# Even layer of a diffusion backbone: two modulation vectors summed over row chunks on VectorE, first attention scores inside the last value block

## Chip, cores and metric

One core of a Trainium2 chip runs the whole kernel in one launch. The metric is the device time of that launch in microseconds (us), median of the runs. The engines are TensorE (PE in the profile), VectorE (DVE), ScalarE (ACT), GpSimd (POOL) and SyncE (SP), which here only issues transfers.

## The reference

Two trunk layers over 256 latent and 256 context tokens of width 1024, all in float32. Each layer is a mixer and then a hierarchical mixture of 32 experts (top 2). Both take their input normalised, scaled and shifted by modulation vectors, and their output is multiplied by a gate vector. There are six vectors a layer, for each of the two streams:

```python
mx = jnp.split((silu_c @ w_mod[l] + b_mod[l])[:, None, :], N_MOD, axis=-1)   # latent stream, c
mc = jnp.split(silu_cc @ w_mod[l] + b_mod[l], N_MOD, axis=-1)                # context stream, c_ctx
hx = rmsnorm(x, norm_mix[l]) * (1.0 + mx[1]) + mx[0]
y_x, y_c = even_mixer(hx, hc, ...)
x = x + mx[2] * y_x
hx = rmsnorm(x, norm_ffn[l]) * (1.0 + mx[4]) + mx[3]
```

`w_mod[l]` is 1024 x 6144, so one vector is a product of two rows (silu of c and of c_ctx) with a 1024 x 1024 matrix of 4 MiB. The even mixer (layer 0) projects `hx` into queries, keys, values and the two halves `u`, `g` of a convolution module. Attention runs over heads of 64; the module computes `u * sigmoid(g)`, a depthwise convolution of 31 taps, a layer norm and silu:

```python
px = hx @ w_in
qx, kx, vx, ux, gx = jnp.split(px, [A_WIDTH, 2 * A_WIDTH, 3 * A_WIDTH, 3 * A_WIDTH + B_WIDTH], axis=-1)
a_x = neighbourhood_attention(heads(qx), heads(kx), heads(vx), kc, vc, rpb)
b_x = conformer_conv(ux * jax.nn.sigmoid(gx))
y_x = jnp.concatenate([a_x, b_x], axis=-1) @ w_out
```

## The kernel before

Each engine has one hand-written stream of instructions, ordered among each other by semaphores. Three structures set the order.

**The ring of weights.** SyncE streams all weights through `ring`, 12 slots of 1 MiB. `slots_before` (L265) gives every load its place; `slot_given_back` (L693) makes the load of slot n wait until slot n - 12 has been used. For slots read by TensorE that is a count on `ring_free`, raised by the first matmul after the use; for slots that VectorE reads it is a count of VectorE's own. A block of the input projection (256 columns) takes one slot, a modulation vector four.

**The plan of PSUM banks.** `psum_plan` (L115) lists every group of matmuls in TensorE's order and deals the eight banks out in turn; scores ("S", n) and transposed probabilities ("PT", n) take two each for four of the units. `open_bank` (L927) makes TensorE wait until the last user of the bank has been drained by ScalarE or VectorE (`act_drained`, `dve_drained`).

**The order of the even layer.** `EVEN_BLOCKS` (L105) are ten blocks: u0, g0, u1, g1, q0, q1, k0, k1, v0, v1. TensorE computes each in two half blocks (L1449). After block 5 (q1) it computes modulation vector 2 (the mixer's gate), after block 8 (v0) vector 3, as 64 matmul instructions over the eight row chunks (`modulation`, L952), with both streams as columns of the weights, and VectorE adds the bias row (L2084). After the ten blocks come 16 units of attention (L1495): transpose of a unit's probabilities (L1474), scores three units ahead (L1445), outputs, and four more modulation vectors. The scores of units 0 and 1 stand before block v0, those of unit 2 before v1 (`FIRST_SCORES`).

VectorE's stream around the change: scale and shift of the input, L2489 copies the shift, L2491 copies the "shift rows" that TensorE then turns, L2492 reduces them, L2495 copies the channel constants. Then the 31 taps of the convolution for two pairs of channel tiles (L2507), each pair 2 tensor-scalar and 60 multiply-adds of 128x512 with both operands in SBUF. Between the pairs it adds vector 2's bias. Then the row maxima of the first units (`maxima`, L2517) and the first normalisation (`normalise`, L2531).

GpSimd's stream (L2877): four gating multiplies z = u * sigmoid(g), each when ScalarE has made the sigmoid; the taps of a pair wait for its two (`gated_in`). Then `mask` (L2719) for four heads, 4 instructions each, on the position bias that `maxima` adds; units 0 to 3 wait for the masks of heads 0 and 1 (`bias_ready`). Then a part of the layer norm, and masks 4 to 7.

In layer 1 one function, `summed` (L2096), already lets VectorE form the products of a vector and TensorE add over partitions only (L967), for the latent stream alone.

## Time and profile before

| | |
|---|---|
| three runs, us | 1002.15, 1003.28, 1004.94; median 1003.28 |
| the profiled execution | 1004.66 us, its span 1002.9 us |
| PE busy | 940.5 us, 94% of the span |
| PE weight loads | 594.7 us, 59% |
| DVE busy | 403.7 us, 40% |
| ACT busy | 247.0 us, 25% |
| POOL busy | 215.1 us, 21% |
| chain that ended last | PE 72%, DMA 13%, DVE 7%, issue 3% |
| largest lines of the chain | L1217 19% and L1017 14% (matmuls), transfers of expert weights 10%, L2503 (the taps) 4% |

The shares are over the whole kernel, of which the even layer's mixer is the first quarter. The time of a change there is read from the stage itself: the chain of waits between about 45 and 320 us and the timelines of the four engines. In the tables of 40 slices the slices 3 to 7 are this stage: TensorE is full in all of them, VectorE is full in most of slices 3 and 5 and nearly idle between.

### The profile page before, as it was taken

How to read it: one execution, taken by the hardware profiler on the slowest of the kernel's cores; microseconds unless marked ns; L12 is line 12 of the kernel's file. 1: busy time of each engine (PE TensorE's matmuls, PEld its weight loads, DVE VectorE, ACT ScalarE, POOL GpSimd, SP SyncE). 2: the span in 40 equal slices, each digit the busy share in tenths (PEclk: the TensorE clock that was granted, in tenths of full speed). 3: DMA queues.
4: the chain of work that ended last, by engine and by line, in shares of the span. 5: the costliest groups of instructions: out<-in, count | busy, mean ns of one | idle time of the engine just before them, and what ended most of it. 6: DMA issues, size and time to landing. Idle time of an engine off the chain costs nothing.

```text
span 1002.9 us, 17308 instructions
## 1 busy us (share of the span) xinstructions
PE 940.5 (94%) x5907; PEld 594.7 (59%) x5908; DVE 403.7 (40%) x887; ACT 247.0 (25%) x538; POOL 215.1 (21%) x309
## 2 busy tenths in 40 slices
PE   5999999999997999998998899999988999999996
PEld 3444448657885555554555475877875555555552
DVE  4149496477546111110111479565344222222124
ACT  4220002465233222221222240132132111111112
POOL 1007501110003233331421000000003333333310
PEclk9999999999997999999999999999999999999999
DMA  9986455799346999999999899893547999999996
GB/s 348 339 239 213 135 174 187 264 326 369 145 165 224 346 404 405 406 405 407 408 406 407 311 381 389 261 325 114 198 167 271 401 399 407 406 403 402 402 407 233
DMA packets 129947, 315.86 MB, mean 315 GB/s; under 512 B 28987, under 2 KB 60755, under 8 KB 129860
## 3 DMA queue, kind: packets, MB, share of 16 engines
q1 hardware_dynamic: 114152, 295.93, 79.5%
q0 software_dynamic: 10800, 12.72, 3.7%
q10 hardware_dynamic: 4908, 6.03, 1.7%
q8 instruction: 57, 0.93, 0.4%
q14 instruction: 30, 0.25, 0.1%
HBM read 315.00 MB, written 22.31 MB: 336 GB/s over the span
## 4 chain that ended last, share of the span: by engine, by line
PE 72%; DMA 13%; DVE 7%; issue 3%; ACT 2%; SPq 2%; POOLq 0%; DVEq 0%; ACTq 0%; POOL 0%
PE ps L1217 19%; PE ps L1017 14%; DMA ring<-in_moe_w 10%; PE ps L1243 9%; PE ps L1069 8%; PE ps L1027 4%; DVE RAB L2503 4%; PE ps L1185 3%; PE ps L960 2%; PE ps L1227 2%; PE ps L1394 1%; SPq L748 1%; DMA mod_rows<-in_norm_ffn 1%; PE ps L1474 1%; PE ps L1490 1%
## 5 line engine op out<-in xcount | busy, mean ns | idle before, releaser
L1217 PE MATMUL ps<-ring,RT 128*64 128x256 f32 x2096 | 253.6, 391 | 17.0 <-DMA ring<-in_moe_w 14.2
L1217 PEld LDWEIGHTS ps<-ring,RT 128*64 128x64 f32 x2096 | 157.4, 140 | 85.9 <-issue 18.4
L1017 PE MATMUL ps<-RT,ring 128*128 128x512 f32 (+1 forms) x544 | 182.1, 493 | 1.1 <-DVE RT L2461 1.1
L1017 PEld LDWEIGHTS ps<-RT,ring 128*128 128x128 f32 x544 | 102.3, 190 | 77.1 <-issue 70.6
L2338 DVE TENSOR_TENSOR RT<-RT,ps 64x256 f32<-64x256 f32 x64 | 27.1, 423 | 261.2 <-ACT RT L1816 153.2
L1243 PE MATMUL ps<-ring,RT 128*64 128x512 f32 x424 | 100.4, 594 | 3.3 <-DVE RT L2344 1.8
L1816 ACT ACTIVATE RT<-ps 64x256 f32<-64x256 f32 x64 | 24.1, 377 | 245.7 <-PE ps L1217 228.7
L2503 DVE SCALAR_TENSOR_TENSOR RAB<-RM,chan,RAB 128x512 f32<-128x512 f32 x120 | 79.7, 748 | 0.0
L2768 POOL DMA_INDIRECT pair_out<-RH,sidx_all x62 | 62.8, 1013 | 55.4 <-POOL sidx_all L2765 50.0
L2744 POOL DMA_INDIRECT RH<-hrow,idx x7 | 7.6, 1085 | 295.9 <-DMA hrow<-RH 294.3
L2756 POOL DMA_INDIRECT RH<-hrow,sidx_all x56 | 59.2, 1057 | 49.4 <-issue 29.9
L1185 PEld LDWEIGHTS ps<-const,RH 128*128 128x128 f32 x252 | 35.3, 209 | 49.4 <-issue 49.4
L1810 ACT ACTIVATE RT<-ps 128x512 f32<-128x512 f32 x64 | 38.2, 597 | 74.8 <-PE ps L1185 70.3
L1027 PE MATMUL ps<-ring,RT 128*128 128x256 f32 x256 | 55.9, 380 | 0.3 <-ACT G L1925 0.3
L1243 PEld LDWEIGHTS ps<-ring,RT 128*64 128x64 f32 x424 | 31.3, 137 | 41.0 <-issue 32.2
L1027 PEld LDWEIGHTS ps<-ring,RT 128*128 128x128 f32 x256 | 48.5, 190 | 8.3 <-issue 1.9
L1185 PE MATMUL ps<-const,RH 128*128 128x128 f32 x252 | 46.9, 310 | 2.9 <-DMA RH<-hrow,idx 1.2
L2344 DVE COPY RT<-ps 128x128 f32<-128x128 f32 x64 | 18.6, 290 | 74.7 <-PE ps L1227 68.4
L2882 POOL TENSOR_TENSOR RM<-RM,PR 128x512 f32<-128x512 f32 x4 | 28.4, 7114 | 74.1 <-ACT PR L1697 74.1
L1069 PE MATMUL ps<-ring,RT 128*128 128x256 f32 x192 | 43.2, 381 | 0.9 <-ACT RT L1697 0.9
L2765 POOL COPY sidx_all<-idx 128x1 int32 (+1 forms) x62 | 11.4, 184 | 149.7 <-ACT RH L1825 67.6
L1069 PEld LDWEIGHTS ps<-ring,RT 128*128 128x128 f32 x192 | 36.0, 190 | 7.2 <-issue 1.4
(314 smaller groups left out, 1039.0 us busy)
## 6 DMA issues: line engine op xcount, KB each, us to landing
ring<-in_moe_w SPq DMA_DIRECT2D x354, 512.0 KB
ring<-in_w_mod SPq DMA_DIRECT2D x96, 512.0 KB
ring<-in_odd_w_in SPq DMA_DIRECT2D x24, 512.0 KB
ring<-in_even_w_in SPq DMA_DIRECT2D x20, 512.0 KB
ring<-in_even_w_out SPq DMA_DIRECT2D x8, 512.0 KB
RAB<-in_moe_w SPq DMA_DIRECT2D x8, 512.0 KB, 8.1
RAB<-pair_out SPq DMA_DIRECT2D x8, 512.0 KB, 9.0
ring<-in_odd_w_out SPq DMA_DIRECT2D x8, 512.0 KB
```

The costliest lines, as they stand in the source:

```text
L1017: mm = pe.matmul(bank, w[:, c, P * ft:P * (ft + 1)], moving[:, c, :], start=(c == 0), stop=(c == NCH - 1))
L1027: mm = pe.matmul(bank[:, BLK * i:BLK * (i + 1)], chunk_of(c, t), w[:, c, :], start=(c == 0), stop=(c == NCH - 1))
L1069: mm = pe.matmul(bank[:, BLK * (b % 2):BLK * (b % 2 + 1)], source[:, c % 4, P * t:P * (t + 1)], w[b][:, c, :], start=(c == 0 and b % 2 == ...
L1185: mm = pe.transpose(ps[:, b, P * j:P * (j + 1)], XG[:, q % 4, j:512:4], ident)
L1217: mm = pe.matmul(bank[CAP * k:CAP * (k + 1), 0:BLK], xt(c), rows_at(w[k], c), start=(c == 0), stop=(c == NCH - 1))
L1243: mm = pe.matmul(bank[CAP * k:CAP * (k + 1), :], ht(f), w[:, D * f + 512 * k:D * f + 512 * (k + 1)], start=(f == 0), stop=(f == 1))
L1810: act.activation(XT[:, b, :, :, :].rearrange("p j a s -> p (j a s)"), ps[:, bank, :], ACT.Copy).then_inc(xT_ready, 1)
L2338: dve.tensor_tensor(HID[:, b, :], SA[:, b, :], ps[CAP:P, 2 + b, 0:BLK], ALU.mult).then_inc(hid_ready, 1)
L2503: return dve.scalar_tensor_tensor(out=out, in0=z, scalar=chan[:, ct, k:k + 1], in1=out, op0=ALU.mult, op1=ALU.add)
L2756: pool.indirect_dma_start(out=XG[:, q % 4, :], out_offset=None, in_=hrow[l], in_offset=bass.IndirectOffsetOnAxis(ap=GIDX[q % 4], axis=0), ...
L2768: pool.indirect_dma_start(out=pair_out[l], out_offset=bass.IndirectOffsetOnAxis(ap=SIDX[b], axis=0), in_=YS[:, b, :], in_offset=None, boun ...
L2882: pool.tensor_tensor(z, z, SG[:, ct % 2, :].rearrange("p (s t) -> p s t", s=2), ALU.mult).then_inc(gated_in, 1)
```

## The change

Vectors 2 and 3 of layer 0 are no longer computed by TensorE over the row chunks. VectorE forms, for each stream, the sum over the eight chunks of weight row times silu value in a 128x1024 tile (`even_vector`: 16 instructions a vector), and TensorE then adds over partitions with 8 matmuls against ones (`even_modulation_of_sums`). VectorE adds the two streams' results into the bias rows, each with a 0/1 factor per partition (`even_modulation`, `of_stream`).

The places move too. Vector 2's weights are loaded behind block 1 and vector 3's behind block 5 (before: 5 and 8). VectorE sums the first half of vector 2 after L2489, its second half after L2492, and vector 3 between the two pairs of taps. TensorE's part comes behind blocks 3 and 7. The ring slots of these vectors are given back by VectorE's count `even_summed`. VectorE finishes vector 2 behind the first pair of taps and vector 3 behind the second. The scores of units 0, 1 and 2 all stand between the two half blocks of v1. With the new list, the banks after v1's first half are: unit 0 in 4 and 5, unit 1 in 6 and 7, unit 2 in 0 and 1, where bank 0 was last used by vector 3.

```diff
--- before.py
+++ after.py
@@ -91,10 +91,12 @@
 
 TILE_ORDER = {4: (1, 0, 3, 2), 2: (1, 0)}
 S_AHEAD = 3
-FIRST_SCORES = {("v", 0): (0, 1), ("v", 1): (2,)}
+FIRST_SCORES = {("v", 1, 1): (0, 1, 2)}
 UNITS = 2 * A_HEADS
 
-MOD_BEHIND = {5: (0, 2), 8: (0, 3)}
+EVEN_SUMMED = [2, 3]
+EVEN_LOADED = {1: 2, 5: 3}
+EVEN_SUMS_BEHIND = {3: 2, 7: 3}
 MOD_ORDER = [(0, 4), (0, 5), (1, 0), (1, 1)]
 
 SUMMED = [2, 4, 3, 5]
@@ -167,12 +169,12 @@
     add(("shift",), "dve")
     add(("chan",), "dve")
     for i, (what, b, _) in list(enumerate(EVEN_BLOCKS))[2:]:
-        for n in FIRST_SCORES.get((what, b), ()):
-            add(("S", n), "act", 2)
         for f in (0, 1):
+            for n in FIRST_SCORES.get((what, b, f), ()):
+                add(("S", n), "act", 2)
             add((what, b, f), "act")
-        if i in MOD_BEHIND:
-            add(("mod",) + MOD_BEHIND[i], "dve")
+        if i in EVEN_SUMS_BEHIND:
+            add(("mod", 0, EVEN_SUMS_BEHIND[i]), "dve")
     for n in range(UNITS):
         add(("PT", n), "act", 2 if n % 4 < 2 else 1)
         if n + S_AHEAD < UNITS:
@@ -268,8 +270,8 @@
     even = []
     for i in range(len(EVEN_BLOCKS)):
         even.append((("in0", i), 1))
-        if i in MOD_BEHIND:
-            even.append((("mod",) + MOD_BEHIND[i], 4))
+        if i in EVEN_LOADED:
+            even.append((("mod0", EVEN_LOADED[i]), 4))
     odd = []
     for i in range(len(ODD_BLOCKS)):
         odd.append((("in1", i), 1))
@@ -284,7 +286,7 @@
 
 def summed_slots(at):
 
-    return {at["mod1", v] + k for v in SUMMED for k in range(4)}
+    return [{at[name, v] + k for v in vs for k in range(4)} for name, vs in (("mod0", EVEN_SUMMED), ("mod1", SUMMED))]
 
 
 
@@ -331,7 +333,8 @@
 def trunk(nc, A):
     plan = psum_plan()
     at = slots_before()
-    by_vector = summed_slots(at)
+    by_vector_of = summed_slots(at)
+    by_vector = by_vector_of[0] | by_vector_of[1]
 
     ctx = ExitStack()
     with ctx:
@@ -416,6 +419,8 @@
                   1: [csilu[:, :, :].rearrange("p c n -> p (c n)"), const[:, C_TRI:C_TRI + BLK], piece[:, :], rt_piece,
                       PR[:, 1, 0:BLK], PR[:, 1, BLK:2 * BLK], wr_pieces[:, 0, :], wr_pieces[:, 1, :]]}
 
+        even_sums = {2: RH[:, 0:2048].rearrange("p (s d) -> p s d", s=2), 3: RAB[:, 0:2048].rearrange("p (s d) -> p s d", s=2)}
+        of_stream = small[:, 212:214]
         row_sums = {2: RH[:, 0:1024], 4: RH[:, 3072:4096], 3: RAB[:, 2048:3072], 5: RAB[:, 3072:4096]}
         back = [RAB[:, 0:2048], RAB[:, 2048:4096], RH[:, 2048:4096], RM[:, 0:2048]]
 
@@ -493,6 +498,7 @@
 
         psum_full = sem("psum_full")
         mod_summed = sem("mod_summed")
+        even_summed = sem("even_summed")
         act_drained = sem("act_drained")
         dve_drained = sem("dve_drained")
         landed = [sem(f"landed{i}") for i in range(RING)]
@@ -694,8 +700,10 @@
 
                 m = n - RING
                 summed = sum(k <= m for k in by_vector)
-                if m in by_vector:
-                    sp.wait_ge(mod_summed, 2 * summed)
+                if m in by_vector_of[0]:
+                    sp.wait_ge(even_summed, 4 * summed)
+                elif m in by_vector:
+                    sp.wait_ge(mod_summed, 2 * (summed - len(by_vector_of[0])))
                 elif m >= 0:
                     sp.wait_ge(ring_free, m + 1 - summed)
 
@@ -880,8 +888,8 @@
                     bias_row(sp, 1)
                     for h in range(4):
                         position_bias(sp, h)
-                if i in MOD_BEHIND:
-                    modulation(MOD_BEHIND[i][0], MOD_BEHIND[i][1:])
+                if i in EVEN_LOADED:
+                    modulation(0, (EVEN_LOADED[i],))
             modulation(0, (4,))
             router_weights(sp, 0)
             sp.dma_start(subln, A["odd_subln"].rearrange("o p -> p o")).then_inc(ld_lam, 16)
@@ -972,6 +980,17 @@
                     mm = pe.matmul(bank[32 * j:32 * j + 32, 0:BLK], ones[:, 0:32], row_sums[v][:, BLK * j:BLK * (j + 1)],
                                    start=True, stop=True)
                     freed(mm)
+                close(mm)
+
+            def even_modulation_of_sums(v):
+
+                bank = open_bank("mod", 0, v)
+                pe.wait_ge(even_summed, 2 * NCH * (EVEN_SUMMED.index(v) + 1))
+                for j in range(4):
+                    for s in (LATENT, CONTEXT):
+                        mm = pe.matmul(bank[32 * j:32 * j + 32, BLK * s:BLK * (s + 1)], ones[:, 0:32],
+                                       even_sums[v][:, s, BLK * j:BLK * (j + 1)], start=True, stop=True)
+                        freed(mm)
                 close(mm)
 
             def warm(name, n):
@@ -1447,11 +1466,11 @@
                 close(mm)
 
             for i, (what, b, _) in list(enumerate(EVEN_BLOCKS))[2:]:
-                for n in FIRST_SCORES.get((what, b), ()):
-                    scores(n)
                 w = slot(at["in0", i])
                 if what == "v":
                     for tp in (0, 1):
+                        for n in FIRST_SCORES.get((what, b, tp), ()):
+                            scores(n)
                         bank = open_bank(what, b, tp)
                         close(by_token(bank, w, (2 * tp, 2 * tp + 1), lambda c, t: hT[:, c, P * t:P * (t + 1)]))
                 else:
@@ -1459,8 +1478,8 @@
                         bank = open_bank(what, b, ft)
                         close(by_feature(bank, w, ft, hT))
                 free(1)
-                if i in MOD_BEHIND:
-                    modulation(*MOD_BEHIND[i], at[("mod",) + MOD_BEHIND[i]])
+                if i in EVEN_SUMS_BEHIND:
+                    even_modulation_of_sums(EVEN_SUMS_BEHIND[i])
 
             def probs_T(n):
 
@@ -1929,9 +1948,9 @@
             for what, b, _ in EVEN_BLOCKS[1:]:
                 if (what, b) == ("v", 0):
                     act.wait_ge(gated_in, 4)
-                for n in FIRST_SCORES.get((what, b), ()):
-                    exps(n)
                 for f in (0, 1):
+                    for n in FIRST_SCORES.get((what, b, f), ()):
+                        exps(n)
                     if what == "u":
                         bank = full(act, what, b, f)
                         drain(Z[:, 2 * b + f, :, PAD:PAD + SEQ], bank.rearrange("p (s t) -> p s t", s=2))
@@ -2093,6 +2112,35 @@
                     dve.scalar_tensor_tensor(out=modrow[:, v, :], in0=modrow[:, v, :], scalar=1.0,
                                              in1=grow[:, v // 4, :], op0=ALU.add, op1=ALU.mult).then_inc(row_scale, 1)
 
+            def even_modulation(v):
+
+                bank = full(dve, "mod", 0, v)
+                for s in (LATENT, CONTEXT):
+                    ins = dve.scalar_tensor_tensor(out=modrow[:, v, :], in0=bank[:, BLK * s:BLK * (s + 1)], scalar=of_stream[:, s:s + 1],
+                                                   in1=modrow[:, v, :], op0=ALU.mult, op1=ALU.add)
+                    if s == LATENT:
+                        step(ins)
+                done(ins)
+
+            def even_vector(v, chunks=range(NCH)):
+
+
+                first, count = at["mod0", v], 2 * NCH * EVEN_SUMMED.index(v)
+                dve.wait_ge(c_silu, 1)
+                for c in chunks:
+                    n = first + c // 2
+                    dve.wait_ge(landed[n % RING], 32 * (n // RING + 1))
+                    w = ring[:, n % RING, D * (c % 2):D * (c % 2 + 1)]
+                    for s in (LATENT, CONTEXT):
+                        sums_of, weight_of_row = even_sums[v][:, s, :], csilu[:, c, s:s + 1]
+                        if c == 0:
+                            ins = dve.tensor_scalar(sums_of, w, weight_of_row, None, ALU.mult)
+                        else:
+                            dve.wait_ge(even_summed, count + 2 * c - 1 + s)
+                            ins = dve.scalar_tensor_tensor(out=sums_of, in0=w, scalar=weight_of_row, in1=sums_of,
+                                                           op0=ALU.mult, op1=ALU.add)
+                        ins.then_inc(even_summed, 1)
+
             def summed(v):
 
 
@@ -2488,9 +2536,13 @@
             dve.wait_ge(z_clear, 1)
             dve.tensor_copy(shift32[:, :, 0:2].rearrange("p (j h) s -> p h j s", h=2),
                             cols[:, 0, 0, :, :, :]).then_inc(shift_copied, 1)
+            for s in (LATENT, CONTEXT):
+                step(dve.tensor_reduce(of_stream[:, s:s + 1], ident.rearrange("p (j k) -> p k j", j=4)[:, s, :], AX.X, ALU.add))
+            even_vector(2, range(NCH // 2))
             done(dve.tensor_copy(shift_rows, full(dve, "shift rows")[:, 0:BLK]))
             done(dve.tensor_reduce(first_shift.rearrange("p (f s) -> p f s", f=2),
                                    full(dve, "shift")[:, 0:16].rearrange("p (f j s) -> p f s j", f=2, j=4), AX.X, ALU.add))
+            even_vector(2, range(NCH // 2, NCH))
             bank = full(dve, "chan")[:, 0:160].rearrange("p (c k) -> p c k", c=4)
             done(dve.tensor_copy(chan[:, :, 0:37], bank[:, :, 0:37]))
 
@@ -2511,8 +2563,9 @@
                         if k:
                             dve.wait_ge(conv_step, 2 * (TAPS * pair + k - 1) + i + 1)
                         tap(2 * pair + i, k).then_inc(conv_step, 1)
+                even_modulation(EVEN_SUMMED[pair])
                 if pair == 0:
-                    modulation(*list(MOD_BEHIND.values())[0])
+                    even_vector(3)
 
             def maxima(n):
 
@@ -2538,10 +2591,7 @@
                 step(dve.tensor_scalar(probs[:, 0, :], probs[:, 0, :], rsum[:, 0:1], None, ALU.mult), wait=False)
                 dve.tensor_scalar(probs[:, 1, :], probs[:, 1, :], rsum[:, 1:2], None, ALU.mult).then_inc(probs_ready, 1)
 
-            for n in FIRST_SCORES["v", 0]:
-                maxima(n)
-            modulation(*list(MOD_BEHIND.values())[1])
-            for n in FIRST_SCORES["v", 1]:
+            for n in range(S_AHEAD):
                 maxima(n)
             normalise(0)
             for n in range(UNITS):
```

## Rows read from the trace of the kernel before

**Rows 1.** The chain of waits, all engines: start us, us, what

```profile
120.04 38.49 DVE RAB L2503 x59
...
162.53 1.28 ACT L1925
163.83 1.45 ACT PR L1925 x4
```

**Rows 2.** TensorE's timeline: start us, us, engine line op, count, idle before

```profile
59.84 55.20 PE L1017 MATMUL ps<-RT,ring 128*128 128x512 f32 x128
114.97 3.66 PE L960 MATMUL ps<-ring,csilu 128*32 128x256 f32 x64
...
146.23 1.99 PE L1445 MATMUL ps<-RH 64*128 64x512 f32 x8
...
166.76 14.05 PE L1027 MATMUL ps<-ring,RT 128*128 128x256 f32 x64 [0.31 <-ACT G L1925]
180.64 1.04 PE L1474 MATMUL ps<-const,PR 128*128 128x128 f32 x8
```

**Rows 3.** VectorE's timeline

```profile
44.23 0.18 DVE L2489 COPY RM<-cols 128x16 f32<-128x16 f32 x1
...
58.33 0.17 DVE L2492 TENSOR_REDUCE small<-ps 128x4 f32<-128x16 f32 x1 [6.95 <-PE ps L1426]
...
64.56 1.00 DVE L2502 TENSOR_SCALAR RAB<-RM,chan 128x512 f32<-128x512 f32 x2 [4.30 <-POOL RM L2882]
65.48 39.83 DVE L2503 SCALAR_TENSOR_TENSOR RAB<-RM,chan,RAB 128x512 f32<-128x512 f32 x60
118.70 0.42 DVE L2090 TENSOR_TENSOR mod_rows<-ps,mod_rows 128x256 f32<-128x256 f32 x1 [13.39 <-PE ps L960]
...
119.95 39.84 DVE L2503 SCALAR_TENSOR_TENSOR RAB<-RM,chan,RAB 128x512 f32<-128x512 f32 x60
...
162.54 0.70 DVE L2527 TENSOR_TENSOR ps<-ps,BIAS 128x512 f32<-128x512 f32 x1
...
164.54 0.17 DVE L2529 TENSOR_SCALAR small<-small 128x2 f32<-128x2 f32 x1
...
166.50 0.69 DVE L2528 TENSOR_REDUCE small<-ps 128x2 f32<-128x512 f32 x1 [0.19 <-PE ps L1445]
...
167.89 0.48 DVE L2539 TENSOR_SCALAR PR<-PR,small 128x512 f32<-128x512 f32 x1
```

**Rows 4.** GpSimd's timeline

```profile
62.15 2.31 POOL L2882 TENSOR_TENSOR RM<-RM,PR 128x512 f32<-128x512 f32 x2 [57.09 <-ACT PR L1697]
81.42 26.07 POOL L2882 TENSOR_TENSOR RM<-RM,PR 128x512 f32<-128x512 f32 x2 [16.97 <-ACT PR L1697]
107.45 0.46 POOL L2725 TENSOR_SCALAR_AFFINE_SELECT BIAS<-BIAS 64x288 f32<-64x288 f32 x1
...
116.38 0.45 POOL L2727 TENSOR_SCALAR_AFFINE_SELECT BIAS<-BIAS 64x288 f32<-64x288 f32 x1
```

**Rows 5.** The source view of line 2882, ns as min/median/max

```profile
L2882 POOL TENSOR_TENSOR RM<-RM,PR x4: 1176/1178/24925, 62.1 to 106.3; 128x512 f32<-128x512 f32 x4
```

**Rows 6.** The chain of waits again, in layer 1: sums over partitions

```profile
650.53 1.43 PE ps L972 x24
```

**Rows 7.** VectorE's groups by line and form, 0 to 300 us: busy us, mean ns

```profile
L2503 DVE SCALAR_TENSOR_TENSOR RAB<-RM,chan,RAB 128x512 f32<-128x512 f32 x120 | 79.7, 748 | 0.0
...
L2110 DVE SCALAR_TENSOR_TENSOR RH<-ring,csilu,RH 128x1024 f32<-128x1024 f32 x7 | 9.0, 1285 | 0.8
...
L2107 DVE TENSOR_SCALAR RH<-ring,csilu 128x1024 f32<-128x1024 f32 x1 | 0.8, 752 | 0.0
```

**Rows 8.** VectorE's timeline at the summed vector of layer 1

```profile
245.95 9.63 DVE L2110 SCALAR_TENSOR_TENSOR RH<-ring,csilu,RH 128x1024 f32<-128x1024 f32 x7
```

**Rows 9.** Busy time by stage, us and instructions; granted clock; DMA

```profile
44.00:48.00 4.00, 4.00 (x10) 1.71 (x9) 0.40 (x3) 1.42 (x4) 0.00 (x0) 1.00 1.05 334
570.00:572.00 2.00, 1.45 (x4) 1.21 (x5) 1.90 (x5) 0.85 (x4) 0.00 (x0) 0.51 0.16 43
```

## The prediction

> **What bounds the kernel now.** The views were read in this order: the chain of waits, TensorE's timeline, VectorE's, GpSimd's, then the source view of one GpSimd line. The chain [rows 1] says that the even layer hangs for 38.49 us on VectorE's taps of the convolution, from 120.04 us, then on the first softmax (table load and exponentials on ScalarE). TensorE's timeline [rows 2] shows the same from the other side: it stands still for only 0.31 us from 59.84 us until the first transpose of probabilities, at 180.64 us, and that wait, ahead of the last value block, is for ScalarE's exponentials, which had waited for the taps: the block's bank is one of the scores'. The end of VectorE's second pair of taps, 119.95 + 39.84 = 159.8 us, and the first transpose, 180.64 us, lie 20.8 us apart. From 180.64 us on TensorE feeds itself through the units; what follows is released by events of this kernel's own order, and the weight stream of the mixture starts again from the gather, so I carry a shift of the first transpose through to the end one to one. So the question is one number: when does the first transpose start?
>
> VectorE is the short resource. Its free time before 159.8 us lies in 44.4 to 64.56 us (small copies only) and 105.3 to 118.70 us, where it waits for TensorE's product for vector 2 [rows 3]. GpSimd uses exactly these two holes: its first two gating multiplies take 2.31 us together from 62.15 us, the next two start at 81.42 us and end at 107.5 us, and the 16 mask instructions run from 107.45 to 116.8 us [rows 4]. The same multiply that takes 1.18 us takes 24.9 us when it starts within the taps [rows 5]: it ended at about 106.3 us, 1 us after the last tap of the pair. While VectorE streams instructions with two operands in SBUF, GpSimd gets nothing.
>
> **What TensorE is relieved of.** Two vectors' products, 64 instructions in 3.66 us each [rows 2], give way to 8 matmuls (16 instructions) each. The nearest row is the sum over partitions of layer 1: 24 instructions in 1.43 us [rows 6], 0.06 us each, so 0.95 us for 16. Here two matmuls in a row go to the same 32 columns, so the upper bound is five steps of a whole matmul at 4 x 0.114 us (3.66/32), 2.3 us. I take 1.2; gain 2.5 us each, 5 us in all, bounds 2.7 to 5.4. It counts only if TensorE is what comes last at 180 us.
>
> **What VectorE gets.** Per vector and stream one scale and seven multiply-adds of 128x1024. The scale is 0.75 us [rows 7]. The multiply-add took 9.63/7 = 1.376 us apiece [rows 8] where each waits for the one before; here two streams alternate, as the taps do. A tap's pitch is 39.83/60 = 0.664 us [rows 3] for 512 columns, 0.084 less than its own 0.748 [rows 7]. Off 1.285 for 1024 columns that leaves 1.20; the scale comes to 0.67. So a vector costs 2 x 0.67 + 14 x 1.20 = 18.1 us, bounds 18.1 and 20.6 (pitch 1.376). Two vectors put 36 us on VectorE.
>
> **Step by step along VectorE.** (1) After the copy of the shift, 44.4 us [rows 3], two tiny reductions (0.4 us, estimate from the 0.17 us of other tiny ones) and the first half of vector 2: 2 x 0.67 + 6 x 1.20 = 8.5, until 53.4 us. Its weights now come ahead of the third input block. The queue moves 334 GB/s [rows 9], 3.1 us a slot of 1.05 MB. Counted in bytes from the start (12.5 MB to the end of the second block, at that rate 37 us) the vector's first two slots are there by about 44 us, where 44.8 and 48.5 are wanted; even 5 us late would cost nothing. TensorE wants the shift rows at 57.8 us, so this half is free; it costs from 58 us on. The third block comes by some 53 us and is wanted at 59.84 us [rows 2]. (2) The second half starts behind the second shift reduction, 58.5 us [rows 3], and takes 8 x 1.20 = 9.6, until 68.1 us. GpSimd's first multiplies arrive at 62.15 us, inside it; by [rows 5] they are held until 68.1 and need 2.31: the taps start at 70.4 us instead of 64.56. (3) A pair of taps: 65.48 + 39.83 - 64.56 = 40.75, until 111.2. (4) Two small multiply-adds finish vector 2, 0.42 each as [rows 3] has it for the addition: 112.1. They read one operand from PSUM, and GpSimd's third multiply, held since 81 us, slips in there (0.3 us of delay). (5) Vector 3 at once: 18.1, until 130.5. Its slots are ordered behind the sixth block and free since 57.9 us. (6) The fourth multiply was held again: 1.15, and the taps wait for it: 131.7. (7) Second pair, 40.75: 172.4 us, against 159.8.
>
> **The masks.** They stand on GpSimd behind the fourth multiply, so the hole that they used is gone: they now fall under the second pair of taps. They are the one operation whose conduct under taps no row shows. Bounds: nothing (they get through), or wholly held as the multiply was. I take held, the nearest row [rows 5]. The first scores wait for masks 0 and 1, 8 instructions with a pitch of (116.38 - 107.45)/15 = 0.595 us [rows 4], last one 0.45: 4.6, so 177.0 us.
>
> **The tail.** First maximum: from the last tap, 159.8, to the start of the second, 162.54, is 2.75: 179.8. Table load and the first unit's exponentials, 162.53 to 165.27 on ScalarE (2.74, [rows 1]): 182.5. Meanwhile the second maximum, 162.54 to 164.71 (2.17), until 182.0; the third and the first normalisation together go from 166.50 to 168.37 (1.87), all [rows 3], and ScalarE is done before the latter is due. The first transpose starts at 183.8 us.
>
> TensorE meanwhile: twelve half blocks at 6.9 (55.20/8) from 59.84 give 142.3; two sums 2.4; three half value blocks at 7.03 (half of 14.05) and two scores 1.99, all [rows 2]: 167.8 us. The third score takes the bank of modulation vector 3, which VectorE empties only behind the second taps: 172.4 + 0.9 = 173.3. This new wait has the score (at most 1.0, half of 1.99) and the last half value block (7.03) queued behind it: 181.3 us, under the 183.8 that the masks give. TensorE's 5 us end in that wait.
>
> **Sum.** 183.8 - 180.6 = +3.2 us. Against its own span of 1002.9 us that is 1006.1, and against the profiled execution's 1004.7 us 1007.9; the median of the three runs shown is 1003.28, and from there the forecast is 1006.5 us. About 0.3%, 3 us, is what a measurement of this kernel can tell from no change.
>
> **A rule against the trace.** In the trace a held multiply stays held over some 36 taps [rows 5]. The Trainium skill, "SBUF — State Buffer", section "Who interferes with whom", says that VectorE and GpSimd share a port pair as an exclusive lock, that a VectorE instruction with two SBUF inputs contends with a GpSimd one that reads SBUF, and that the loser blocks until the other's instruction is finished. By that the multiply would have had its turn after one tap; the trace agrees with the lock, not with its length. What turns would do here is rival 3.
>
> **Rivals.**
> 1. Masks get through under the taps at no cost. Then the bank is what comes last: 181.3 us, +0.7: 1004.0. For it: masks cover half the partitions and no row shows them held. Against: they read and write SBUF as the multiply does.
> 2. GpSimd is not held by the sums at all. The taps start at 68.6, no wait at (6), no masks late: second pair ends at 169.2, bank at 170.1, end of the last half block at 178.1 us: -2.5, 1000.8. Against it stands the 24.9 us. If TensorE were last as well and the sums cheap, the floor is 167.8 + 1.0 + 7.0 = 175.8, -4.8: 998.5.
> 3. GpSimd takes turns. Then all 16 masks (0.45 each, 7.2) and two multiplies (2.3) come out of VectorE's stream, less the 1.15 of step (6) and the 0.3: 180.5, bank 181.4, first transpose 189.4: +8.8, 1012.1. It is worse because the stream has no hole left; it decides as soon as VectorE ends after 173. The lasting hold of 24.9 us speaks against it.
> 4. TensorE's clock. It stands idle from 168 to 173.3 us. [rows 9] has a stretch in which it came back from standing idle and 0.51 was granted, the lower level of 1.2 GHz. Half speed for 3 us costs 1.5: 182.8 us, still under 183.8 and so nothing; for the whole of the last half block it costs 7, 188.3 us: +7.7, 1011.0.
> 5. The sums run at the pitch of 1.376: 22 of them stand on the path, 22 x 0.176 = 3.9 more: 1010.4.
>
> **How the numbers follow.** Forecast 42%; it straddles the bound of 3 us, so 26 go to slower and 16 to same. Rival 1 14%, same. Rival 2 17%, of which 9 same and 8 faster, and 3% for its floor, faster. Rivals 3, 4 and 5 with 8, 9 and 7%, slower. That is 11% faster, 39% same, 50% slower. The range reaches from rival 2 to just about rivals 4 and 5: 1000.2 to 1010.5 us. The forecast's own range is 1005 to 1008.
>
> **What would show it.** In the profile after: first tap at 70 us and not 64.6; two GpSimd multiplies stretched to 6 us and one to 30; masks spread or starting only near 172 us; second pair of taps ending near 172; TensorE idle before the third score for some 5 us and again before the first transpose. The prediction is wrong if the masks are done before 172 us, if the multiply-adds have another pitch than 1.20, or if a shift of the first transpose isn't found again at the start of the mixture.

## The result and the profile after

The changed kernel takes 1008.85 us (median of 5 runs, 1008.54 to 1011.21) against 1003.29 us of the kernel before on the same chip: 1.0055 times, 95% interval 1.0035 to 1.0076. It is slower by 5.6 us. The profiled execution took 1011.21 us, its span is 1009.5 us. The page's first part, busy time by engine:

```profile
PE 937.2 (93%) x5811; PEld 592.1 (59%) x5812; DVE 448.1 (44%) x923; ACT 247.9 (25%) x538; POOL 235.8 (23%) x309
```

TensorE lost 3 us of work, VectorE gained 44 (448.1 - 403.7). This profile starts late: the copy of the shift, which stands ahead of all that is changed, is at 45.13 us where [rows 3] has 44.23. So 0.9 us comes off every time of after before it is held against the rows of before. VectorE's timeline, which answers [rows 3]:

```profile
45.13 0.18 DVE L2537 COPY RM<-cols 128x16 f32<-128x16 f32 x1
...
46.93 7.26 DVE L2140 SCALAR_TENSOR_TENSOR RH<-ring,csilu,RH 128x1024 f32<-128x1024 f32 x6
...
59.76 11.49 DVE L2140 SCALAR_TENSOR_TENSOR RH<-ring,csilu,RH 128x1024 f32<-128x1024 f32 x8 [0.34 <-issue]
...
72.43 39.84 DVE L2555 SCALAR_TENSOR_TENSOR RAB<-RM,chan,RAB 128x512 f32<-128x512 f32 x60
112.18 1.01 DVE L2119 SCALAR_TENSOR_TENSOR mod_rows<-ps,small,mod_rows 128x256 f32<-128x256 f32 x2
113.10 2.35 DVE L2137 TENSOR_SCALAR RAB<-ring,csilu 128x1024 f32<-128x1024 f32 x2
115.37 19.48 DVE L2140 SCALAR_TENSOR_TENSOR RAB<-ring,csilu,RAB 128x1024 f32<-128x1024 f32 x14
134.78 1.28 DVE L2554 TENSOR_SCALAR RAB<-RM,chan 128x512 f32<-128x512 f32 x2
135.97 39.82 DVE L2555 SCALAR_TENSOR_TENSOR RAB<-RM,chan,RAB 128x512 f32<-128x512 f32 x60
175.72 0.99 DVE L2119 SCALAR_TENSOR_TENSOR mod_rows<-ps,small,mod_rows 128x256 f32<-128x256 f32 x2
```

From 59.76 us to the end of vector 3 at 176.7 us VectorE has no hole left. The six multiply-adds of the first half run at 1.21 us each, the eight of the second half at 1.44, the fourteen of vector 3 at 1.39. GpSimd's timeline (answering [rows 4]) tells why the latter two are longer:

```profile
63.06 3.52 POOL L2932 TENSOR_TENSOR RM<-RM,PR 128x512 f32<-128x512 f32 x2 [58.00 <-ACT PR L1716]
82.34 32.56 POOL L2932 TENSOR_TENSOR RM<-RM,PR 128x512 f32<-128x512 f32 x2 [15.75 <-ACT PR L1716]
114.85 0.91 POOL L2775 TENSOR_SCALAR_AFFINE_SELECT BIAS<-BIAS 64x288 f32<-64x288 f32 x1
115.91 1.24 POOL L2777 TENSOR_SCALAR_AFFINE_SELECT BIAS<-BIAS 64x288 f32<-64x288 f32 x1
...
135.31 0.46 POOL L2777 TENSOR_SCALAR_AFFINE_SELECT BIAS<-BIAS 64x288 f32<-64x288 f32 x1
```

The first two multiplies get through inside the second half of vector 2. The sixteen masks don't come under the second taps: fifteen of them run inside vector 3's sum, one for each of VectorE's instructions (both have a pitch of 1.39 us), and the last in the scale behind it. TensorE's timeline, answering [rows 2]:

```profile
144.57 1.09 PE L991 MATMUL ps<-RAB,const 128*32 128x256 f32 x16
145.59 20.99 PE L1046 MATMUL ps<-ring,RT 128*128 128x256 f32 x96
166.51 1.99 PE L1464 MATMUL ps<-RH 64*128 64x512 f32 x8
176.76 1.23 PE L1464 MATMUL ps<-RH 64*128 64x256 f32 x4 [8.27 <-DVE mod_rows L2119]
177.92 8.66 PE L1046 MATMUL ps<-ring,RT 128*128 128x256 f32 x32
186.42 1.04 PE L1493 MATMUL ps<-const,PR 128*128 128x128 f32 x8
...
190.10 3.66 PE L968 MATMUL ps<-ring,csilu 128*32 128x256 f32 x64
```

Here is the loss. The third score stands still for 8.27 us until VectorE has emptied vector 3's bank (L2119), and the last half value block stands behind it. The first transpose is at 186.42, less 0.9 is 185.5 us, against 180.64 before: +4.9 us. The stage table of after (busy us and instructions of PE, PEld, DVE, ACT, POOL; then the granted clock, DMA share, GB/s) adds that the stop also cost the clock:

```profile
168.00:172.00 4.00, 0.50 (x4) 0.00 (x0) 4.00 (x7) 0.52 (x1) 0.00 (x0) 0.84 0.00 0
172.00:176.00 4.00, 0.00 (x0) 0.00 (x0) 4.00 (x7) 0.00 (x0) 0.06 (x1) 0.50 0.00 0
176.00:180.00 4.00, 3.23 (x9) 2.23 (x10) 3.81 (x6) 0.17 (x1) 3.70 (x3) 0.50 0.00 0
180.00:184.00 4.00, 4.00 (x17) 3.44 (x17) 3.76 (x8) 3.19 (x11) 0.00 (x0) 0.88 0.00 0
```

The granted clock fell during the stop and was still 0.50 when work began again. At 0.50, the lower level of 1.2 GHz, the score takes 1.23 us instead of 0.70 and the block 8.66 instead of 7.17 (both found at full clock in a run below).

### The profile page after: what moved, and what is told of

It reads as the page before. It is cut to its first block, busy times and chain, and to the rows that moved or that the text cites. A ratio compares the mean times of both kernels' runs of the same rounds, so it can differ in the third digit from the quotient of the medians.

```text
span 1009.5 us, 17166 instructions
## 1 busy us (share of the span) xinstructions
PE 937.2 (93%) x5811; PEld 592.1 (59%) x5812; DVE 448.1 (44%) x923; ACT 247.9 (25%) x538; POOL 235.8 (23%) x309
## 4 chain that ended last, share of the span: by engine, by line
PE 67%; DVE 14%; DMA 11%; issue 3%; SPq 2%; ACT 2%; POOLq 0%; DVEq 0%; POOL 0%; ACTq 0%
PE ps L1236 19%; PE ps L1036 10%; PE ps L1262 9%; PE ps L1088 8%; DMA ring<-in_moe_w 8%; DVE RAB L2555 8%; PE ps L1046 4%; PE ps L1204 3%; PE ps L968 2%; PE ps L1246 2%; SPq L756 2%; DMA RH<-hrow,sidx_all 2%; PE ps L1413 1%; DMA ring<-in_w_mod 1%; DVE RAB L2140 1%
## 5 line engine op out<-in xcount | busy, mean ns | idle before, releaser
L1236 PE MATMUL ps<-ring,RT 128*64 128x256 f32 x2096 | 254.0, 391 | 18.0 <-DMA ring<-in_moe_w 15.1
L1236 PEld LDWEIGHTS ps<-ring,RT 128*64 128x64 f32 x2096 | 157.3, 140 | 87.3 <-issue 19.0
L1036 PEld LDWEIGHTS ps<-RT,ring 128*128 128x128 f32 x544 | 102.2, 190 | 77.2 <-issue 70.6
L2818 POOL DMA_INDIRECT pair_out<-RH,sidx_all x62 | 63.5, 1024 | 55.4 <-POOL sidx_all L2815 51.7
L2932 POOL TENSOR_TENSOR RM<-RM,PR 128x512 f32<-128x512 f32 x4 | 36.1, 9042 | 73.8 <-ACT PR L1716 73.8
```

The costliest lines, as they stand in the source:

```text
L1036: mm = pe.matmul(bank, w[:, c, P * ft:P * (ft + 1)], moving[:, c, :], start=(c == 0), stop=(c == NCH - 1))
L1236: mm = pe.matmul(bank[CAP * k:CAP * (k + 1), 0:BLK], xt(c), rows_at(w[k], c), start=(c == 0), stop=(c == NCH - 1))
L2818: pool.indirect_dma_start(out=pair_out[l], out_offset=bass.IndirectOffsetOnAxis(ap=SIDX[b], axis=0), in_=YS[:, b, :], in_offset=None, boun ...
L2932: pool.tensor_tensor(z, z, SG[:, ct % 2, :].rearrange("p (s t) -> p s t", s=2), ALU.mult).then_inc(gated_in, 1)
```

## The experiments

All runs of this section stand in one table. "Ratio" is to the kernel before in the same set of runs, with its 95% interval. "Stage" is read from the profile: from the copy of the shift on VectorE to the start of the first product behind the transposes on TensorE (vector 4's; in after 190.10 - 45.13 = 144.97), which leaves out start-up and all that follows. "Against before" is its difference to before's 140.09 (184.32 - 44.23). The kernel after ran in the first set alone, so runs that start from it are held against it by stage.

| run | what is different | median us (runs) | ratio | stage us | against before |
|---|---|---|---|---|---|
| before | | 1003.2 to 1003.9 (5 to 29) | 1 | 140.09 | |
| after | | 1008.85 (5) | 1.0055 (1.0035 to 1.0076) | 144.97 | +4.9 |
| v2_only | after, vector 3 as before | 998.74 (12) | 0.9959 (0.9942 to 0.9975) | 136.97 | -3.1 |
| v2_only_early | that, scores placed as before | 1001.16 (11) | 0.9987 (0.9972 to 1.0002) | 137.53 | -2.6 |
| scores_late_only | before, scores placed late | 1003.59 (12) | 1.0003 (0.9987 to 1.0019) | 139.55 | -0.5 |
| scores_early | after, scores placed as before | 1022.49 (4) | 1.0186 (1.0145 to 1.0227) | 157.61 | +17.5 |
| own_bank | after, vector 3 in bank 3 | 1010.76 (6) | 1.0073 (1.0046 to 1.0101) | 145.63 | +5.5 |
| warm | after, matmuls fill the wait | 1005.94 (12) | 1.0035 (1.0014 to 1.0056) | 142.94 | +2.9 |
| early_sum | after, two chunks summed earlier | 1003.53 (10) | 1.0008 (0.9985 to 1.0030) | 140.66 | +0.6 |
| halves | after, sums in tiles of 512 | 1014.82 (4) | 1.0114 (1.0086 to 1.0142) | 148.48 | +8.4 |
| no_masks | after, masks 0 to 3 left out | 1014.63 (4) | 1.0122 (1.0087 to 1.0157) | 142.32 | +2.2 |
| masks_first | before, masks ahead of two multiplies | 1003.23 (10) | 0.9998 (0.9981 to 1.0016) | 140.03 | -0.1 |
| later1, later3 | before, third multiply a little later | 1003.58, 1002.72 (one run each) | | 140.10, 140.10 | 0.0 |

### Which part costs: one vector, or the place of the scores

v2_only takes from after all that belongs to vector 3 and leaves it on TensorE behind block 8. The lists say it; the loops that read them follow:

```diff
-EVEN_SUMMED = [2, 3]
-EVEN_LOADED = {1: 2, 5: 3}
-EVEN_SUMS_BEHIND = {3: 2, 7: 3}
+EVEN_SUMMED = [2]
+EVEN_LOADED = {1: 2, 8: 3}
+EVEN_SUMS_BEHIND = {3: 2}
```

> Only vector 2 is summed by VectorE; vector 3 goes back to TensorE behind block v0, its weights are loaded there, late scores stay. Theory (VectorE's 22 us for vector 3 between the pairs of taps is what comes last, TensorE's relief is real but hidden): the second pair of taps ends near 155 us (175.8 with both sums), no bank waits on it, TensorE is last again and keeps one vector's saving of 2.6 us, so 1000.7 us, faster than both kernels. Rival (the sums are cheap and the late place of the scores costs the time): stays above 1005 us. On GpSimd's masks, which now fall under the second pair of taps with nothing else there: if taps hold them as they hold the multiply, they start only near 155 us; if they get turns there as they did among the 1024-column sums (one each 1.39 us), they run from 114 to 136 us and the taps' pitch rises from 0.664 us.

VectorE's timeline of v2_only:

```profile
115.97 42.48 DVE L2559 SCALAR_TENSOR_TENSOR RAB<-RM,chan,RAB 128x512 f32<-128x512 f32 x60
162.44 0.42 DVE L2113 TENSOR_TENSOR mod_rows<-ps,mod_rows 128x256 f32<-128x256 f32 x1 [3.98 <-PE ps L970]
170.58 0.70 DVE L2583 TENSOR_TENSOR ps<-ps,BIAS 128x512 f32<-128x512 f32 x1 [7.72 <-PE ps L1466]
```

The second taps end at 158.45 us, and afterwards it waits for TensorE, 3.98 and 7.72 us: the order of the two engines is turned round. TensorE's own rows have no wait between 144.80 us and the transposes:

```profile
162.30 7.17 PE L1048 MATMUL ps<-ring,RT 128*128 128x256 f32 x32
169.40 2.42 PE L1466 MATMUL ps<-RH 64*128 64x512 f32 x12
171.75 7.17 PE L1048 MATMUL ps<-ring,RT 128*128 128x256 f32 x32
```

The transposes follow at 178.76 us. The stage is 3.1 us shorter than before. Vector 2's product explains 2.6 of it (3.66 - 1.09), and the wait of 0.31 us for ScalarE [rows 2] that is gone makes 2.9. This is the fastest version of the study, faster than both kernels: 5.1 us by the medians, of which the stage explains 3.1 (the interval reaches from 2.5 to 5.8). Between it and after lie 8.0 us of stage, and what moves with vector 3 makes them: a stop of 8.27, the clock's 0.5 on the score and 1.5 on the block, less 2.57 that TensorE no longer computes, is 7.7.

The place of the scores was put back in both forms of the kernel, and moved alone in the kernel before. The edit of scores_late_only is this line (and the loops that read it), the other two go the other way:

```diff
-FIRST_SCORES = {("v", 0): (0, 1), ("v", 1): (2,)}
+FIRST_SCORES = {("v", 1, 1): (0, 1, 2)}
```

> The kernel before with one part of the change alone: the scores of units 0, 1 and 2 stand between the two half blocks of v1; both vectors stay with TensorE. Theory (their place is free as long as VectorE is done with the taps by 160 us): the 0.31 us wait ahead of the last value block goes, the first normalisation is ready near 178.3 us and the transposes start at 180.3 us: within 0.3% of the kernel before, 1003.0 us. Rival (maxima, exponentials and normalisation have too little cover behind 7 us of matmuls): first transpose 2 us later or more, 1005.5 us.

> The kernel with only vector 2 on VectorE, with the first scores back in their old places (units 0 and 1 ahead of v0, unit 2 ahead of v1). It prices the late place where VectorE is ahead. Theory: the taps end at 158.5 us, the exponentials of unit 1 at 165.5 us, and the last value block, whose bank they hold, could start at 163.9 us: 1.5 us of TensorE waiting come back, 1000.3 us. Rival (the place is free here as well): no difference, 998.7 us.

> The changed kernel with the first scores in their old places (units 0 and 1 ahead of v0, unit 2 ahead of v1), both vectors on VectorE. Theory (whatever of the value blocks stands behind a bank that VectorE empties after the second taps is added to the time): the third score's wait for the bank of vector 3 now has the whole last value block behind it, 14.05 instead of 7.03 us, so 7 us later than the changed kernel, less what of the half clock it absorbs: 1015 us. Rival (the late scores are what costs, since their softmax stands bare): faster than the changed kernel, near 1004 us.

Alone it moves nothing that can be measured. With one vector the stage gains 0.6 us, where 1.5 us of waiting were expected: the last value block waited 0.30 us with the scores in their old place. The medians are 2.4 us apart, but the two intervals touch and the profiles show the difference behind the stage, so only the 0.6 us is read as the edit's. With both vectors it is worth 12.6 us of stage. TensorE's rows of scores_early:

```profile
178.66 1.23 PE L1464 MATMUL ps<-RH 64*128 64x256 f32 x4 [15.23 <-issue]
184.52 16.55 PE L1046 MATMUL ps<-ring,RT 128*128 128x256 f32 x64 [4.63 <-ACT PR L1944]
```

The third score waits here too until VectorE is through (its last copy of vector 3 ends at 178.56 us), but now with both halves of v1 behind it, and the first of these waits 4.63 us more for exponentials of ScalarE, since its bank is a score's. The direction was expected, the size was not: 1015 was forecast and 1022.5 measured, as neither the second wait nor the lower clock (0.50 from 168 to 188 us) was in the sum.

### Is it the bank?

own_bank gives vector 3 a bank of its own turn, so that the third score needn't wait for it:

```diff
-            add(("mod", 0, EVEN_SUMS_BEHIND[i]), "dve")
+            add(("mod", 0, EVEN_SUMS_BEHIND[i]), "dve", bank=3 if i == 7 else None)
```

> The changed kernel with modulation vector 3 in bank 3, which no score or value block needs before unit 4; nothing else moves. Theory (the third score's wait for that bank and the last half value block behind it are what comes last at 186.4 us): TensorE ends the value block near 176 us, the first transpose then waits for VectorE's normalisation, which ended at 184.0 us in the changed kernel: 2.3 us earlier, less up to 1.6 us if the granted clock is at half when the transposes begin, since TensorE then stands idle right ahead of them: 1006.6 to 1008.2 us. Rival (VectorE's chain alone sets the time, the bank does not matter): 1008.8 us and the first transpose at the same place behind the last tap, 10.6 us.

TensorE's timeline of own_bank:

```profile
170.47 7.17 PE L1046 MATMUL ps<-ring,RT 128*128 128x256 f32 x32
185.76 1.94 PE L1493 MATMUL ps<-const,PR 128*128 128x128 f32 x8 [8.11 <-DVE PR L2592]
187.63 1.23 PE L1464 MATMUL ps<-RH 64*128 64x256 f32 x4
188.78 1.97 PE L1493 MATMUL ps<-const,G 128*128 128x128 f32 x8
190.68 1.78 PE L1464 MATMUL ps<-RH 64*128 64x512 f32 x4
```

The bank wait is gone and the value block done at 177.6 us, yet nothing is won; the forecast of a small gain missed. TensorE stands still for 8.11 us one step later, until VectorE has normalised the first probabilities. The transposes begin 2.3 us earlier than in after (139.0 against 141.3 from the shift's copy), and that is given back: they and the scores between them now run at the lower clock (0.72 from 180 us, 0.50 from 184 us), 6.9 us for the four rows that take 4.0 in after (1.04, 0.70, 1.09, 1.13). So the bank is where the wait shows, not what causes it. The cause is that VectorE's stream ends late.

### What the stop costs beyond itself

warm puts 36 matmul instructions without use (8.04 us) between the second and third score. They end before the bank comes free, so the wait stays as long and only TensorE's clock can change:

```diff
+                            if n == 2:
+                                warm(("v", 1, 1), 18)
                             scores(n)
```

> The changed kernel with 18 extra 128x256 matmuls on TensorE, into the bank of the last half value block, in the idle time ahead of the third score (8.27 us idle there; they need 7.7 us). Theory (1.9 us of the loss is the clock at 0.5 over the third score and the start of the last half value block, 1.23 and 8.66 us for 0.70 and 7.03): granted clock stays 1.00, the half block takes 7.03 us and the time falls by 1.9 us, to 1007.0 us. Rival (the slow stretch is hidden, since the normalisation comes as late anyway): below 0.5 us of change. If the extra matmuls outlast the wait, up to 1 us is lost.

TensorE's timeline of warm, behind the added matmuls:

```profile
175.50 0.70 PE L1464 MATMUL ps<-RH 64*128 64x256 f32 x4 [0.29 <-DVE mod_rows L2121]
176.13 7.17 PE L1046 MATMUL ps<-ring,RT 128*128 128x256 f32 x32
```

The score starts at the same distance from the shift's copy (131.62 us, in after 131.63). It and the block now take 0.70 + 7.17 instead of 1.23 + 8.66, with 1.00 granted throughout, and the stage is 2.0 us shorter. The lower clock is 2.0 of the 4.9 us.

### Is it VectorE's stream, one to one?

Between the copy of the shift rows (54.5 us in after) and the reduction at 59.24 VectorE waits 4.71 us. early_sum does two more chunks of vector 2 there; the work is the same, only the hole is filled:

```diff
             done(dve.tensor_copy(shift_rows, full(dve, "shift rows")[:, 0:BLK]))
+            even_vector(2, range(4, 6))
...
-            even_vector(2, range(NCH // 2, NCH))
+            even_vector(2, range(6, NCH))
```

> The changed kernel with chunks 4 and 5 of vector 2 summed ahead of the second shift reduction, in 4.7 us in which VectorE stood idle, and only 6 and 7 behind it. Theory (VectorE's stream up to the last tap is the path, one to one): the reduction comes about 1 us later, the first taps start 3.9 to 4.8 us earlier, the second taps end as much earlier, and TensorE's wait ahead of the third score falls from 8.3 to about 4 us: 4 us faster than the changed kernel, 1004.9 us, 5 with the clock kept. Rival (something beside VectorE's stream holds the first transpose): less than 2 us.

VectorE's timeline of early_sum, second pair of taps:

```profile
129.53 39.83 DVE L2556 SCALAR_TENSOR_TENSOR RAB<-RM,chan,RAB 128x512 f32<-128x512 f32 x60
```

The second taps end at 169.36 - 43.71 = 125.65 us from the shift's copy, in after at 130.66: 5.0 us earlier. TensorE's wait at the third score falls from 8.27 to 3.26 us, also 5.0; the block behind it is 0.7 us longer (9.37), still at the lower clock, which leaves 4.3 us of stage. What VectorE ends earlier comes off the end one for one, less the clock. With both vectors on VectorE the kernel is then as fast as before (1.0008, interval 0.9985 to 1.0030).

### GpSimd inside VectorE's stream

no_masks leaves out the masks of heads 0 to 3 and only raises their semaphore:

> The changed kernel without the mask instructions of heads 0 to 3, so the position bias stays unmasked for them. Theory (masks cut into vector 3's sum: 16 of them and 14 steps with a pitch of 1.39 instead of 1.20 us): vector 3 takes 18.5 instead of 21.7 us, the taps end 3 us earlier and the time falls by 3 us to 1005.9 us, somewhat more if the granted clock no longer falls ahead of the third score. Rival (the sums' pitch has another cause, such as the waits on landed weights): pitch stays 1.39 us, no change of time.

VectorE's timeline of no_masks, vector 3's sum and the scale of the taps behind it:

```profile
114.50 16.82 DVE L2140 SCALAR_TENSOR_TENSOR RAB<-ring,csilu,RAB 128x1024 f32<-128x1024 f32 x14
131.24 0.99 DVE L2554 TENSOR_SCALAR RAB<-RM,chan 128x512 f32<-128x512 f32 x2
```

Without masks fourteen multiply-adds take 16.82 us, a pitch of 1.20; with them 19.48. Masks cost VectorE 2.66 us there and 0.29 in the scale behind, 0.19 a mask, which itself takes 0.45 alone. The stage falls by 2.65 us, as VectorE's row says. The whole time doesn't: unmasked scores change what the kernel computes, and behind 700 us layer 1's mixture runs 1056 matmul instructions at L1236 with weights from the ring where after has 1024. Other choices of experts would explain it. Its total tells nothing of the masks and is left aside.

halves asks whether the width of VectorE's instructions decides who is held. Its sums are in tiles of 512 columns, as the taps are (the instructions then take `w[:, half]`, and the counts that are waited for double):

```diff
-                    for s in (LATENT, CONTEXT):
-                        sums_of, weight_of_row = even_sums[v][:, s, :], csilu[:, c, s:s + 1]
+                    for s, h in ((LATENT, 0), (CONTEXT, 0), (LATENT, 1), (CONTEXT, 1)):
+                        half = slice(512 * h, 512 * (h + 1))
+                        sums_of, weight_of_row = even_sums[v][:, s, half], csilu[:, c, s:s + 1]
```

> The changed kernel with each 1024-column step of the sums as two of 512 columns, four sums in turn; order and data otherwise the same. It asks why GpSimd got turns among the sums (one mask each 1.39 us, a multiply 0.6 us longer than alone) but its multiply was held for 30 us under the taps. Theory width: between instructions of 512 columns a two-operand multiply gets no turn, so the first two multiplies are held until the second half of vector 2 is through, and the fourth until vector 3 is. Rival (the sums differ from the taps in something else, their waits on landed weights or where they read): the multiplies get turns as before, 3.5 us for the pair. Either way the sums take 2 x 0.664 = 1.33 for 1.20 us, and 22 of them stand on the path: about 3 us slower than the changed kernel, 1011.5 us; some 2 us less if the first two multiplies no longer cut in.

The first two multiplies get through under these sums as well, 2.97 us for both (3.52 in after, 2.31 alone). Width alone is not what decides. The kernel is slower still, since vector 3's 28 multiply-adds take 21.30 us.

masks_first is the kernel before with the masks between the second and third multiply, and no longer behind the fourth. It asks whether masks are let in among taps, and what becomes of a multiply that comes behind them:

```diff
             for b in (0, 1):
+                if b:
+                    for h in range(4):
+                        mask(h)
```

> The kernel before, with GpSimd's masks of heads 0 to 3 ahead of its third and fourth multiply; they become due near 68 us, inside the first pair of taps. Theory kind of instruction (a one-operand select gets a turn between taps, the two-operand multiply does not): the 16 masks run from about 68 us with a pitch near 0.85 us until 82 us, the taps' pitch rises to 0.70 us meanwhile, and the multiply behind them is held as before. Rival who was first (what arrives in a running stream of taps is held, whatever it is): the first mask is stretched to some 37 us and ends at 106 us. Time of the kernel: both leave it within 0.3% of before, since VectorE has 13.4 us of waiting behind this pair; in the rival case the masks end at 116 and the multiplies at 118.5 us, just at the start of the second pair.

GpSimd's timeline of masks_first, the last mask and the third and fourth multiply:

```profile
75.99 0.71 POOL L2727 TENSOR_SCALAR_AFFINE_SELECT BIAS<-BIAS 64x288 f32<-64x288 f32 x1
81.05 1.20 POOL L2885 TENSOR_TENSOR RM<-RM,PR 128x512 f32<-128x512 f32 x1 [4.34 <-ACT PR L1697]
87.84 21.83 POOL L2885 TENSOR_TENSOR RM<-RM,PR 128x512 f32<-128x512 f32 x1 [5.59 <-ACT PR L1697]
```

Masks get their turns under the taps, at 0.71 us each instead of 0.45. Then the third multiply, which was held for 24.93 us in before, took 1.20 us in the middle of a row of 60 taps (65.22 to 108.64 us), and the fourth, in the same row, 21.83 us. So neither the kind of instruction nor its operands hold it by themselves. VectorE's timeline shows what the turn cost it, the tap before and the tap that waited:

```profile
80.48 0.74 DVE L2503 SCALAR_TENSOR_TENSOR RAB<-RM,chan,RAB 128x512 f32<-128x512 f32 x1
81.14 1.66 DVE L2503 SCALAR_TENSOR_TENSOR RAB<-RM,chan,RAB 128x512 f32<-128x512 f32 x1
```

That is 0.92 us for a multiply, against 0.2 for a mask. The whole time doesn't move: VectorE had the room.

later1 and later3 ask for the moment of arrival. One (later1) or three (later3) tiny writes stand ahead of the third multiply of the kernel before:

```diff
+                    for _ in range(1 if ct == 2 else 0):
+                        step(pool.memset(small[:, 214:215], 0.0))
```

> The kernel before with one tiny memset (128x1) on GpSimd right ahead of its third multiply, so that the multiply reaches the running taps some 0.1 to 0.3 us later. Theory (whether an arrival in a running stream of taps gets a turn depends on the moment): with this or the next delay it gets through in about 1.2 us, as it did behind the masks, and only the fourth is held. Rival (the third multiply is held whenever no GpSimd work ran under this pair of taps before): held for 24.9 us again in both. No change of time.

> As the run before with three memsets in a chain, a delay of some 0.4 to 0.9 us. Same two theories: through in 1.2 us in at least one of the two delays, or held in both.

GpSimd's third and fourth multiply, of later1 and then of later3:

```profile
82.55 25.92 POOL L2884 TENSOR_TENSOR RM<-RM,PR 128x512 f32<-128x512 f32 x2
82.48 25.60 POOL L2884 TENSOR_TENSOR RM<-RM,PR 128x512 f32<-128x512 f32 x2
```

Held against the start of the tap that was running, the multiply arrived 0.04 us into a tap in before, 0.20 in later1, 0.51 in later3 and 0.64 in after, and in early_sum the same multiply 0.34. It is held in all five, until the taps are over. The fourth of masks_first, held too, arrived 0.48 us in. But the one that got through arrived at 0.57 (81.05 - 80.48), and every mask that got its turn between taps (masks_first, v2_only) arrived 0.53 to 0.54 us in, where no held multiply did: the nearest are 0.51 and 0.63 (v2_only). So the moment of arrival isn't ruled out; the two delays missed the stretch that would tell. It is hardly all, since among the 512-column sums of halves a multiply that arrived 0.39 us into an instruction got through. What the sums have otherwise, such as that they don't read RM, the tile that the multiply writes and the taps read, wasn't tested. What holds the multiply stays open.

## Why the prediction came out as it did

The forecast was 1006.5 us, +3.2, from one first transpose; measured are +5.6 and, for the transpose, +4.9. The measured time lies in the wide range (1000.2 to 1010.5) and outside the forecast's own (1005 to 1008). The direction, the stage and the two chains that could come last were right. Which of them does was wrong: the forecast rests on masks held under the second taps, and by its own sign ("wrong if the masks are done before 172 us") it failed there, since they were done at 134.9. With the masks as they were and all else as forecast, its sum would have been the bank's way, 181.3 us or +0.7, which is the time of rival 1. The measured +4.9 is that 0.7 plus 2.5 from VectorE and 1.9 from the clock, less 0.2 of overlap. That this comes out near +3.2 is luck: a delay that never came stood in for two that weren't in the sum. Times of after less 0.9 us.

**VectorE up to vector 2, steps 1 to 4: right.** First half until 53.3 us (53.4 forecast), first tap pair begins at 70.6 (70.4) and ends at 111.4 (111.2), vector 2 finished at 112.3 (112.1). The pitch of 1.20 us was measured as 1.21 and 1.20. The two multiplies were not held until the sum's end but took turns in it; they cost it 1.9 us instead of 2.31 behind it, so the sum hid the error.

**Step 5, vector 3 in 18.1 us: 3.65 us too short.** It took 21.75 us and ended at 133.95 (130.5, with 0.3 us of delay that didn't come). The sum assumed that nothing of GpSimd comes in. The fourth multiply (0.93 us, the two scales took 2.35 instead of the first half's 1.42) and the masks (2.66 in no_masks) did. In return step 6, a wait of 1.15 us for that multiply, fell away: the taps began without one. Second taps end at 174.9 us instead of 172.4: **+2.5**.

**The masks: wrong by 4.6 us the other way.** They were taken as held under the second taps, with one multiply's row [rows 5] as the nearest, and were to delay the first scores by 4.6 us. They were done in the very stretch before. The bounds were "nothing" and "wholly held"; it was a price between, 0.19 us of VectorE each. Rival 3 had the turns but at 0.45 us a mask, and put two multiplies on top, hence its 1012.1. That "GpSimd gets nothing" while VectorE streams two operands was a reading of one row, and the masks contradict it. Rule and row part here: by the Trainium skill, "SBUF — State Buffer", section "Who interferes with whom", the loser blocks until the other's instruction is finished. The masks did just that, one turn an instruction; the third multiply was held over some 45 taps (31 us) in after. Either conduct occurs, so a single row of one of them was no basis for the other instruction.

**Which comes last at the transpose: wrong.** Forecast: the first normalisation at 183.8, the bank's way at 181.3. Measured: the normalisation at 183.1 (184.04 - 0.9), the bank's way 185.5 us. TensorE didn't stand idle a second time ahead of the first transpose, as it would have with the normalisation last. In the normalisation's chain the masks' 4.6 us were missing and the 2.5 of VectorE came on; its rest is longer by 1.4, of which 0.9 is vector 3's finish at L2119, which the sum charged to the bank but not to the maxima behind it on the same engine, and 0.4 is L2582 (1.19 us where the same instruction took 0.76 before). The table load was no part of it: ScalarE's rows of after show it right behind its last drain, 12.6 us before the first exponential. The third row is VectorE's, the end of the first normalisation.

```profile
167.23 1.28 ACT L1944 ACT_TABLE_LOAD   x1
179.83 0.69 ACT L1944 ACTIVATE PR<-ps,small 128x512 f32<-128x512 f32 x1 [11.32 <-DVE small L2582]
183.56 0.48 DVE L2592 TENSOR_SCALAR PR<-PR,small 128x512 f32<-128x512 f32 x1
```

**The clock, rival 4: right mechanism, wrong cover.** It was said to cost 1.5 us, by an assumed 3 us at half speed, hidden under the 183.8. It cost 2.0 us (warm), and as the bank's way came last nothing hid it. The two errors of this way, VectorE's 2.5 and the 1.9 by which score and block took longer than 1.0 + 7.03, are the 4.2 us from 181.3 to 185.5 within the 0.2 by which rows overlap.

**TensorE's gain: as said.** A sum takes 1.09 us (1.2 forecast), 2.57 less than a product, and both gains end in the wait. (Twelve half blocks of 6.9 from 59.84 give 142.6 and not the 142.3 of the sum; TensorE then waits until 173.3 all the same, so the forecast doesn't move.) v2_only shows the same gain counted in full as soon as VectorE is not last.

**Carrying the shift through: right as far as the mixture.** The matmul at L1106 of before, which stands ahead of layer 0's mixture, is at 307.70 us; in after (L1125) it is at 313.47, or 4.9 us later with the 0.9 taken off. The span grew by 5.7 without the start's 0.9. The remaining 0.8 us says little: from the same matmul on, masks_first, in which nothing behind the stage is changed, is 3.7 us shorter than before in its profile, and v2_only 4.8 us shorter than its stage explains. The cause of these differences is open. Own_bank and halves have 1.0 and 1.8 us more at that matmul than in the stage, in the attention; that too is open. In all runs but halves and no_masks the stage's difference lies within the interval of the whole time.

## What to carry to other kernels

Work that moves to an engine with holes fits as long as the holes last: here one vector gained 0.4% and the second, the same edit, turned it into a loss of 0.5%. With one, VectorE has 11.7 us of waiting left behind the taps (3.98 and 7.72); the second takes 21.75 us. (The second vector alone on VectorE wasn't run.) Add up the receiving engine's stream to its last consumer, other engines' turns included, before adding up what the giving engine saves. If a wait on a buffer disappears when the buffer is changed and comes back one step later, a late producer is the likely cause; end the producer earlier, as early_sum does, to see it.

## What the runs showed of the hardware

- GpSimd beside VectorE's instructions with two SBUF operands: masks of 64x288 got one turn for each VectorE instruction, costing it about 0.2 us (both for 1024 and 512 columns: 2.64 us for 13 in the taps of v2_only, 42.48 - 39.84). A multiply of 128x512 that got its turn cost it 0.92. Among taps that happened once, in 1.20 us; in all other cases the multiply was held for 21.8 to 31.6 us. Among the sums it got its turn each time, with 1024 and with 512 columns. What decides is open.
- TensorE, idle for 8.3 us, was granted 0.50 for the 4 us after it, and its next 7.87 us of work took 9.89. In own_bank, after 8.1 us idle, transposes and scores that take 4.0 us took 6.9.
- Sums over partitions into 32 columns: 16 instructions in 1.09 us, 0.07 each, although two in a row go to the same columns.
- ScalarE's table load stood ahead of the wait for the maxima in every kernel where the exponential follows a drain, and behind it (162.53 us in [rows 1]) in every kernel where it follows the separate wait on `gated_in`, so the late scores also hide 1.28 us.
